# Block 2's gate products spread over its attention, with weights laid out by block and conditioning units moved

## The chip, the cores and the metric

The program runs on one core of a Trainium2 chip. Its time is the device time of one launch in microseconds (us). The engines that matter are TensorE (PE, matrix products; its weight loads are listed as PEld), VectorE (DVE), ScalarE (ACT), GpSimd (POOL) and SyncE (SP), which issues the weight loads from memory. TensorE's clock has two levels, 1.2 and 2.4 GHz; the granted clock in the rows is the share of full speed.

## The reference

Two transformer blocks run on 256 tokens of width 2048, all in fp32. Block 1: attention with a relative bias beside a pooling branch, output projection, then an up projection whose result passes a causal depthwise convolution of three taps, gelu times value, and a down projection. Block 2 is conditioned: a vector gives shifts, scales and gates through the large matrix `w_ada`.

```python
p = h @ w_in_l                              # keys, values, queries and 2 x 2048 gate columns
oa = gqa(qa, ka_all, va_all)                # 16 heads of 128, keys of context and tokens (512)
ob = diff_attn(qb, kb_all, vb_all, ...)     # 8 heads, each two softmaxes over 512 keys
merged = sigmoid(g_a) * (oa @ w_br_a) + sigmoid(g_b) * (ob @ w_br_b)
x = x + m_lat[2] * (merged @ w_out)
x = x + m_lat[5] * ((silu(h @ w_ff_gate) * (h @ w_ff_up)) @ w_ff_down)
```

## The kernel before

The kernel keeps the activations on chip, features on the partitions, and streams every weight once. A stage (`Stage`, L96) is one weight matrix or a part of it; its groups are blocks of 256 output columns, and a group is cut into units of 512 rows by 256 columns (512 KB). A unit goes through a ring of four buffers: SP loads `raw` (L374), ACT rounds it to `whi` (`hi`, L540), DVE forms the rest `wlo` (`lo`, L850), and PE does 24 products for the unit (`multiply`, L1330 to L1334), which together give an fp32 result. `raw` of a slot may be loaded again when its `wlo` is done, `whi` may be overwritten when PE has used the slot's previous unit. So the order of work on every engine is the order of units that the code writes out, and one late link holds the units behind it.

Some stages also carry conditioning items (`ada=1`): each body of two or four groups gets four extra units of `w_ada` in the ring (`ADA_AFTER`, L50). Three of them are scaled by ACT (L536, four instructions each) and added up by POOL (L408 to L419); the fourth is done by DVE alone (L842, L845). Then PE sums over partitions (L1343) and DVE stores the item (`store_mods`, L979). There are 64 items.

In the up projections DVE takes a finished group out of PSUM (L924), and applies the taps (L931 newest, L936 the two older ones, for two tiles of 128 channels each), all of it ahead of the next `lo` in DVE's order; gelu (L548) and the product with the value half follow (L968 to L974).

Between the query stage `q_rest` and the gate stages nothing is multiplied with streamed weights: key and query norms (PE L1513 and L1497, ACT L719, DVE L1224), rotations (ACT swaps L742, DVE L1214 to L1218, POOL L511 to L513), then 32 units of attention a (score L1540, maximum L1252, exp L763, scale L1248, transposes L1525, copy L771, values L1532) and 16 units of attention b (score L1567, maximum L1275, two exps L787, L1262 to L1270, copy L795, values). Then the sums for the output norm of attention b (PE L1588, one ACT square root L805) are formed, and the stages `gate_a` and `gate_b` run: 16 groups of 4 units, with 8 conditioning items. ACT writes their sigmoids (L551) to on-chip tiles. In `gate_a` DVE also normalizes the heads of b (`output_norm`, with two reciprocals a body). `branch_a` and `branch_b` follow, then `out`. PSUM has four banks `acc` (two groups of two), two `turned`, `sums` and `ada_sums`.

Of the kernel before, what the change touches and what calls it, by code (L numbers as in the profile page):

```python
# [32 lines left out]
P = 128  # L33
# [61 lines left out]
V_STEPS = {"scale": 0, "mix_out": 3, "conv": (6, 9), "down1": 0, "down2": 3, "kv": 0, "q": 0, "gate": 0,  # L95
           "branch_a": 0, "branch_b": 1, "out": 4, "glu": (0, 3), "down_x": 3}  # L96
A_STEPS = {"conv": (1, 0), "gate": (1, 1), "glu": (2, 1)}
# [26 lines left out]
def build(nc, xT, ctxT, vec, cst, rel, w_in, pool_w, w_o, w_up, w_down, w_ada, w_in2, w_bra, w_brb, w_out2,  # L124
          w_fg, w_fu, w_fd, out):
    km = lambda w: w.rearrange("(k p) n -> p k n", p=P)
    W = {k: km(v) for k, v in dict(w_in=w_in, w_o=w_o, w_up=w_up, w_down=w_down, w_in2=w_in2, bra=w_bra, brb=w_brb,
                                   out=w_out2, fg=w_fg, fu=w_fu, fd=w_fd).items()}
    ada_src = km(w_ada)

    def cols(w, k, c0, stride):

        return lambda b, GB, gb, u: W[w][:, k + UK * u:k + UK * u + UK, ds((b * GB + gb) * stride + c0, GW)]

    def pairs(wg, wu, g0, u0):

        return lambda b, GB, gb, u: W[(wg, wu)[gb % 2]][:, UK * u:UK * u + UK,
                                                          ds(b * GW + (g0, u0)[gb % 2], GW)]
# [6 lines left out]
    st_up1b = Stage("up1b", pairs("w_up", "w_up", 4 * GW, DFF + 4 * GW), 2 * n1 - 8, 4, "conv", tile0=8, feat0=8)  # L145
# [6 lines left out]
    st_ga = Stage("gate_a", cols("w_in2", 0, KVW + QW, GW), 8, 4, "gate", ada=1, tile0=16)  # L152
    st_gb = Stage("gate_b", cols("w_in2", 0, KVW + QW + D, GW), 8, 4, "gate", ada=1, tile0=48)
    st_ba = Stage("branch_a", cols("bra", 0, 0, GW), 8, 4, "branch_a", ada=1, op=88)
    st_bb = Stage("branch_b", cols("brb", 0, 0, GW), 8, 2, "branch_b", per_body=4, ada=1, who=1)
    st_out = Stage("out", cols("out", 0, 0, GW), 8, 4, "out", op=104)
# [5 lines left out]
    stages = number([st_in, st_o, st_up1a, st_up1b, st_dn1, st_up2, st_dn2, st_kv, st_q1, st_q2, st_ga, st_gb, st_ba, st_bb,  # L162
                     st_out, st_u1a, st_u1b, st_d1, st_u2, st_d2])

    with ExitStack() as ctx:
# [27 lines left out]
        CA = sb("cond_sums", [P, 2, GW], F32, here(2 * GW * 4))  # L193
        IO = sb("ident_ones", [P, 256], F32, here(1024))
# [17 lines left out]

        PS = ctx.enter_context(nc.psum_tensor("acc", [P, 2, 2, 512], F32))
# [55 lines left out]
        split_hi = sem("split_hi")  # L269
        out_stored = sem("out_stored")  # L270
# [24 lines left out]
        def cond_silu(st, u, x):  # L295

            k = (KT if st.ib >= ADA_CTX else 0) + UK * u + x
            return CS[:, k:k + 1]

# [54 lines left out]
        O_SRC = (8, 12, 32, 36)  # L354

# [4 lines left out]
        def _(sp):  # L360
            def load(st, b, prior):

                for j, (gb, u) in enumerate(st.entries):
                    if gb is None:
                        src = ada_src[:, UK * u:UK * u + UK,
                                      ds((b + st.ib) * GW - (ADA_CTX * GW if st.ib >= ADA_CTX else 0), GW)]
                    else:
                        src = st.src(b, st.GB, gb, u)
# [24 lines left out]
        def _(pool):  # L393
# [75 lines left out]
            add_condition(st_up1a)  # L469

# [23 lines left out]
            pool.wait_ge(ada_ops, st_ga.ib * ADA_OPS + 1)  # L494
# [19 lines left out]
            for st in (st_ga, st_gb, st_ba, st_bb, st_u1a):  # L514
# [4 lines left out]
        def _(act):  # L519
# [23 lines left out]
            def post(st, b, gb):  # L543

                g = group(st, b, gb)
                if st.kind == "conv" and gb % 2 == 0:
                    act.wait_ge(evac_done, g + 3)
                    act.activation(Gb[:], Cb[:], ACT.Gelu_apprx_tanh).then_inc(astep, 1)  # L548
                elif st.kind == "gate":
                    act.wait_ge(used, grouped(st, b, gb))  # L550
                    act.activation(R[:, ds(b * 4 + (st.tile0 + 2 * gb), 2), :], PS[:, gb % 2, :, 0:S],  # L551
                                   ACT.Sigmoid).then_inc(astep, 1)
# [5 lines left out]
            def gate_act(st, b):  # L558

                act.wait_ge(evac_done, group(st, b, 0) + 3)  # L560
                act.activation(Gb[:], Gb[:], ACT.Silu).then_inc(astep, 1)

            def body(st, b, final=False):

                for j in range(RING, RING + st.upb):
# [9 lines left out]
                    if st is st_ga and j == RING + 8:  # L575
# [1097 lines left out]
```

## Time and profile before

| | |
|---|---|
| median of 3 runs | 3146.78 us (3143.88 to 3147.21) |
| profiled execution | 3145.76 us, span 3143.9 us |
| PE, PEld busy | 2926.2 us (93%), 2699.2 us (86%) |
| DVE, ACT, POOL busy | 62%, 50%, 25% |
| moved from memory | 598.29 MB, mean 190 GB/s, most of it in packets of about 1 KB |
| mean granted PE clock | 0.97 |

A busy PE is not a PE at its peak: ends of products are modelled, so the number of products in a stretch says more than the busy share. Times in the rows are counted from the span's start. Rows of a stretch give the busy time of each engine with the number of its instructions. Rows of groups give line, engine, operation, output and input with shapes and count, then busy time, the mean of one in ns, and the idle time just before them with who ended it. An fp32 product that is not split by hand shows as two records.

### The profile page before, as it was taken

To read this page: it belongs to the slowest core of one execution; us is meant where nothing else is said; L and a number is where in the kernel's file an instruction comes from. 1 tells how busy PE (TensorE), PEld (TensorE's weight loads), DVE (VectorE), ACT (ScalarE), POOL (GpSimd) and SP (SyncE) were. 2 spreads that over 40 slices of the span, in tenths; PEclk is the share of its full clock that TensorE was granted. 3 is DMA by queue.
4 is the path that set the end of the run, shared out by engine and by line. 5 is a ranking of instruction groups with operands and counts; after the bars stand their busy time and mean duration, and the time that the engine had idled before them with its cause. 6 is when DMAs were issued, how large, how long until landed. Compare 5 with 4: busy or idle time off the path is not lost.

```text
span 3143.9 us, 57610 instructions
## 1 busy us (share of the span) xinstructions
PE 2926.2 (93%) x20282; PEld 2699.2 (86%) x20282; DVE 1946.6 (62%) x2412; ACT 1564.1 (50%) x2203; POOL 786.3 (25%) x646
## 2 busy tenths in 40 slices
PE   7998789999998997999998778999997999999999
PEld 7988789999988997788898547999996888888888
DVE  5566888776688866433456555655766665555554
ACT  5555554345565543323455645665535644334443
POOL 2554432003233321212341402445303400000000
PEclk9999899999999998999998989999998999999999
DMA  7874666657777764344574003887755865656655
GB/s 245 266 246 126 222 201 201 180 181 243 240 225 227 235 218 148 120 149 135 180 248 140 1 1 125 255 261 247 241 182 178 255 213 181 188 186 187 187 185 163
DMA packets 595176, 598.29 MB, mean 190 GB/s; under 512 B 18257, under 2 KB 593105, under 8 KB 594833
## 3 DMA queue, kind: packets, MB, share of 16 engines
q1 hardware_dynamic: 591936, 589.37, 60.3%
q10 hardware_dynamic: 2368, 4.91, 0.4%
q0 software_dynamic: 784, 2.88, 0.3%
q8 instruction: 50, 0.82, 0.1%
q14 instruction: 38, 0.30, 0.0%
HBM read 594.99 MB, written 2.10 MB: 190 GB/s over the span
## 4 chain that ended last, share of the span: by engine, by line
PE 60%; DVE 15%; DMA 10%; ACT 7%; issue 7%; DVEq 1%; ACTq 0%; SPq 0%
PE acc L1334 19%; PE acc L1330 13%; PE acc L1332 13%; PE acc L1333 12%; DVE wlo L850 5%; DMA raw<-w_ada 5%; DMA raw<-w_in 2%; ACT whi L540 2%; ACT cond_products L536 1%; DVE cond_sums L842 1%; DVE conv_out L936 1%; PE sums L1392 1%; DMA raw<-w_up 1%; DMA raw<-w_brb 1%; DVE conv_in L924 1%
## 5 line engine op out<-in xcount | busy, mean ns | idle before, releaser
L850 DVE TENSOR_TENSOR wlo<-raw,whi 128x1024 fp32r<-128x1024 f32 x864 | 1120.3, 1307 | 892.5 <-ACT whi L540 888.9
L1334 PE MATMUL acc<-operand,wlo 128*128 128x256 f32 (+1 forms) x5504 | 1606.6, 292 | 0.0
L540 ACT ACTIVATE whi<-raw 128x1024 fp32r<-128x1024 f32 x864 | 911.3, 1058 | 1096.5 <-PE acc L1334 733.5
L1332 PE MATMUL acc<-operand,whi 128*128 128x256 f32 (+1 forms) x4096 | 1222.6, 298 | 98.3 <-DVE wlo L850 63.4
L1333 PE MATMUL acc<-operand,whi 128*128 128x256 f32 (+1 forms) x4096 | 1210.7, 296 | 0.0
L1334 PEld LDWEIGHTS acc<-operand,wlo 128*128 128x128 f32 x5504 | 1063.0, 193 | 15.4
L1332 PEld LDWEIGHTS acc<-operand,whi 128*128 128x128 f32 x4096 | 795.4, 194 | 125.4 <-DVE wlo L850 56.5
L1333 PEld LDWEIGHTS acc<-operand,whi 128*128 128x128 f32 x4096 | 795.6, 194 | 15.0
L408 POOL TENSOR_TENSOR cond_products<-cond_products 128x512 f32<-128x512 f32 x192 | 252.6, 1316 | 1425.9 <-ACT cond_products L536 1424.0
L1330 PE MATMUL acc<-operand,whi 128*128 128x512 f32 x1408 | 502.9, 402 | 16.9 <-DVE wlo L850 9.0
L536 ACT ACTIVATE cond_products<-raw,cond_silu 128x256 f32<-128x256 f32 x768 | 327.8, 498 | 255.7 <-PE acc L1334 159.3
L1334 PE MATMUL acc<-ffn_act,wlo 128*128 128x256 f32 x1408 | 396.9, 282 | 0.0
L1330 PEld LDWEIGHTS acc<-operand,whi 128*128 128x128 f32 x1408 | 266.3, 189 | 86.9 <-DVE wlo L850 12.9
L1334 PEld LDWEIGHTS acc<-ffn_act,wlo 128*128 128x128 f32 x1408 | 268.1, 190 | 0.0
L1330 PE MATMUL acc<-ffn_act,whi 128*128 128x512 f32 x704 | 248.8, 399 | 0.0
L1332 PE MATMUL acc<-ffn_act,whi 128*128 128x256 f32 x704 | 200.2, 284 | 4.6 <-DVE wlo L850 4.6
L1333 PE MATMUL acc<-ffn_act,whi 128*128 128x256 f32 x704 | 199.2, 283 | 0.0
L416 POOL TENSOR_TENSOR cond_sums<-cond_sums,cond_products 128x256 f32<-128x256 f32 x128 | 163.3, 1276 | 10.0
L1330 PEld LDWEIGHTS acc<-ffn_act,whi 128*128 128x128 f32 x704 | 132.3, 188 | 33.0
L414 POOL TENSOR_TENSOR cond_products<-cond_products 128x256 f32<-128x256 f32 x128 | 151.1, 1181 | 10.0
L1332 PEld LDWEIGHTS acc<-ffn_act,whi 128*128 128x128 f32 x704 | 135.1, 192 | 5.8 <-DVE wlo L850 5.8
L1333 PEld LDWEIGHTS acc<-ffn_act,whi 128*128 128x128 f32 x704 | 135.1, 192 | 0.0
(201 smaller groups left out, 2000.0 us busy)
## 6 DMA issues: line engine op xcount, KB each, us to landing
raw<-w_ada SPq DMA_DIRECT2D x256, 512.0 KB, 4.7
raw<-w_in SPq DMA_DIRECT2D x224, 512.0 KB, 4.8
raw<-w_up SPq DMA_DIRECT2D x176, 512.0 KB, 4.8
raw<-w_down SPq DMA_DIRECT2D x88, 512.0 KB, 4.9
raw<-w_fg SPq DMA_DIRECT2D x88, 512.0 KB, 4.3
raw<-w_fu SPq DMA_DIRECT2D x88, 512.0 KB, 4.5
raw<-w_fd SPq DMA_DIRECT2D x88, 512.0 KB, 3.5
raw<-w_o SPq DMA_DIRECT2D x32, 512.0 KB, 4.8
```

The costliest lines, as they stand in the source:

```text
L408: pool.tensor_tensor(w[:, 0:2, :], w[:, 0:2, :], w[:, 2:4, :], ALU.add).then_inc(ada_ops, 1)
L414: pool.tensor_tensor(w[:, 0, :], w[:, 0, :], w[:, 1, :], ALU.add).then_inc(ada_ops, 1)
L416: pool.tensor_tensor(CA[:, 1, :], CA[:, 1, :], w[:, 0, :], ALU.add).then_inc(ada_ops, 1)
L536: ins = act.activation(prod[j % RING][:, x, :], raw[j % RING][:, x, :], ACT.Copy, scale=cond_silu(st, u, x))
L540: act.activation(whi[j % RING][:], raw[j % RING][:], ACT.Copy).then_inc(hi_done, 2 if st.entries[j % st.upb - 1] == (None, ADA_VEC) else 1)
L842: ins = dve.scalar_tensor_tensor(out=CA[:, 0, :], in0=w, scalar=c, in1=CA[:, 0, :], op0=ALU.mult, op1=ALU.add)
L850: dve.tensor_tensor(wlo[j % RING][:], raw[j % RING][:], whi[j % RING][:].bitcast(F32), ALU.subtract).then_inc(lo_done, 2 if prev[0] is Non ...
L924: did(dve.tensor_tensor(Zp[:, :, 2:S + 2], sums, rep(RS[:], 2), ALU.mult))
L1330: pe.matmul(both, h[:, x, f], mov, start=first, stop=False)
L1332: pe.matmul(out_, h[:, x, f], mov[:, 0], start=first, stop=False)
L1333: pe.matmul(out_, h[:, x, f], mov[:, 1], start=False, stop=False)
L1334: ins = pe.matmul(out_, l[:, x, f], mov[:, 0], start=False, stop=last)
```

## The change

1. `gate_a` and `gate_b` become one stage `gates` of 16 groups without conditioning, and its 64 units are written out as 64 slots. In slot s, PE first does a piece of the norms (slots 2 to 9), of attention a (slots 11 to 45) or of attention b (slots 43 to 61), then the 24 products of unit s. ACT and DVE do the same one slot ahead, with the split of unit s + 4 first. The gate sums use two PSUM banks instead of four, scores the other two. Attention b's scores have one buffer instead of two. Attention outputs go to `sums` and `ada_sums`.
2. Every fourth slot ACT takes the sigmoid of a group into a small tile `GT` and issues a store to memory (16 of 256 KB). Ahead of `branch_a` ACT issues four loads of 1 MB that bring them back; DVE waits for two of them ahead of `branch_a`'s splits, for the rest ahead of `branch_b`'s.
3. The output norm of attention b moves behind the slots: its sums are inserted after the first unit of `branch_a`, the reciprocals and splits into `branch_a`'s bodies.
4. The 8 conditioning items of the gates move to the next four bodies of block 1's up projection (`up1b`) and to `out`.
5. In all up projections the newest tap (with the bias) moves from DVE to ACT; DVE does its `lo` before the older taps.
6. The host stores each weight matrix by blocks of 256 columns, so a unit is 4 KB contiguous for each partition instead of four pieces of 1 KB.

```diff
-V_STEPS = {..., "conv": (6, 9), ...
+V_STEPS = {..., "conv": (4, 7), ...
-A_STEPS = {"conv": (1, 0), "gate": (1, 1), "glu": (2, 1)}
+A_STEPS = {"conv": (2, 1), "glu": (2, 1)}
...
+    def block_of(w, g, k):
+        return W[w][:, ds(g, 1), k:k + UK, :].rearrange("p g k c -> p (g k) c")
...
+    st_up1b = Stage("up1b", ..., 8, 4, "conv", ada=1, tile0=8, feat0=8)
+    st_up1c = Stage("up1c", ..., 2 * n1 - 16, 4, "conv", tile0=16, feat0=16)
-    st_ga = Stage("gate_a", ..., 8, 4, "gate", ada=1, tile0=16)
-    st_gb = Stage("gate_b", ..., 8, 4, "gate", ada=1, tile0=48)
+    st_g = Stage("gates", ..., 16, 4, "gate")
+    st_out = Stage("out", ..., 8, 4, "out", ada=1, op=104)
...
+        gates = nc.dram_tensor("gates_spilled", (P, 32, S), F32).ap()
... scalar
+            def newest_tap(st, b, gb):
+                act.wait_ge(vstep, vst(st, b, gb, 0))
+                for m in range(2):
+                    ins = act.activation(Cb[:, m, :], Zp[:, m, 2:S + 2], ACT.Identity, scale=V[:, ds(t2 + m, 1)],
+                                         bias=V[:, ds(tb + m, 1)])
...
+            def gate(g):
+                act.wait_ge(used, grouped(st_g, g // 2, g % 2))
+                if g:
+                    act.wait_ge(gate_out, 16 * g)
+                act.activation(GT[:], PS[:, 0, g % 2, :]..., ACT.Sigmoid).then_inc(evac_done, 1)
+            for s in SLOTS:
+                hi(...)                      # unit s + 4
+                if s % 4 == 0 and s:
+                    spill(s // 4 - 1)
+                norms(s)
+                attend_a(s + 1 - AT_A)       # copy, exp, output; AT_A = 11
+                attend_b(s + 1 - AT_B)       # AT_B = 43
+                if s % 4 == 3:
+                    gate(s // 4)
... vector
+            for s in SLOTS:
+                lo(...)                      # unit s + 4
+                norms(s)                     # key scaling, rotations
+                attend_a(s + 1 - AT_A)       # maximum, then the scaling of the unit before
+                attend_b(s + 1 - AT_B)
+            dve.wait_ge(in_ga, 32)
             run(st_ba)
+            dve.wait_ge(in_gb, 32)
             run(st_bb)
... tensor
+            for s in SLOTS:
+                if 2 <= s < 2 + NK:
+                    broadcast(s - 2)
+                if s in SUMS_AT:
+                    head_sums(NK + SUMS_AT[s])
+                attend_a(s - AT_A)           # transposes of n-2, values of n-3, score of n
+                attend_b(s - AT_B)
+                multiply(st_g, b, j, False)
+            body(st_ba, 0, insert=0)         # output_sums() behind the first unit
... host
+    by_block = lambda w: np.ascontiguousarray(
+        w.reshape(w.shape[0] // P, P, w.shape[1] // GW, GW).transpose(1, 2, 0, 3))
```

## Rows read from the trace of the kernel before

**Rows 1.** Six stretches: us, busy (x records) by engine, PE clock, DMA share, GB/s.
```profile
600.00:650.00 50.00, 50.00 (x419) 50.00 (x418) 37.84 (x58) 19.85 (x20) 0.00 (x0) 1.00 0.59 179
838.15:1116.45 278.30, 253.08 (x2004) 249.59 (x2004) 230.81 (x301) 167.00 (x236) 100.98 (x92) 0.96 0.73 228
1687.40:1918.00 230.60, 175.71 (x977) 123.89 (x975) 130.35 (x258) 132.76 (x255) 33.57 (x22) 0.86 0.03 8
1918.00:2021.50 103.50, 99.14 (x807) 98.34 (x808) 66.97 (x67) 69.15 (x100) 41.79 (x36) 0.98 0.75 234
2021.50:2116.70 95.20, 91.86 (x763) 91.35 (x761) 53.23 (x54) 58.38 (x89) 45.62 (x36) 1.00 0.85 264
2116.70:2146.50 29.80, 28.10 (x222) 28.13 (x223) 19.27 (x20) 16.46 (x24) 11.80 (x9) 0.94 0.68 209
```

**Rows 2.** PE in order of time: first scores, then one unit of attention a.
```profile
1724.41 3.76 PE L1540 MATMUL acc<-tiles 128*128 128x512 f32 x4
...
1809.86 0.66 PE L1525 MATMUL turned<-ident_ones,operand_scratch 128*128 128x128 f32 x4
...
1811.21 1.05 PE L1532 MATMUL acc<-operand_scratch,tiles 128*128 128x128 f32 x8
1812.27 0.66 PE L1525 MATMUL turned<-ident_ones,operand_scratch 128*128 128x128 f32 x4
```

**Rows 3.** PE in order of time: one unit of attention b.
```profile
1856.83 0.66 PE L1525 MATMUL turned<-ident_ones,operand_scratch 128*128 128x128 f32 x4 [0.28 <-DVE operand_scratch L1270]
1857.42 1.13 PE L1567 MATMUL acc<-tiles 64*128 64x512 f32 x4
1858.48 1.16 PE L1532 MATMUL sums<-operand_scratch,tiles 128*128 128x128 f32 x8
```

**Rows 4.** Groups on ACT between 1687.4 and 1918 us.
```profile
L763 ACT ACTIVATE operand_scratch<-acc,small,operand_scratch 128x512 f32<-128x512 f32 x32 | 24.9, 778 | 28.2 <-DVE small L1255 28.0
L787 ACT ACTIVATE operand_scratch<-acc,small,operand_scratch 128x512 f32<-128x512 f32 x32 | 24.6, 772 | 36.9 <-DVE small L1278 36.9
L771 ACT ACTIVATE operand_scratch<-turned 128x512 f32<-128x512 f32 x32 | 18.8, 586 | 0.7 <-PE turned L1525 0.7
L742 ACT ACTIVATE operand_scratch<-tiles 64x1024 f32<-64x1024 f32 x8 | 8.4, 1056 | 0.1
L787 ACT ACTIVATION_READ_ACCUMULATOR operand_scratch<-acc,small,operand_scratch 128x1 f32 x32 | 6.2, 193 | 0.0
```

**Rows 5.** Groups on ACT in the two gate stages.
```profile
L540 ACT ACTIVATE whi<-raw 128x1024 fp32r<-128x1024 f32 x64 | 67.3, 1056 | 47.1 <-DMA raw<-w_in 39.3 <-POOL cond_sums L416 4.5 <-DMA raw<-w_bra 2.1
...
L551 ACT ACTIVATE tiles<-acc 128x512 f32 x16 | 9.3, 583 | 0.0
...
L551 ACT ACT_TABLE_LOAD x4 | 5.1, 1283 | 0.1
```

**Rows 6.** Groups on DVE between 1687.4 and 1918 us.
```profile
L1252 DVE TENSOR_REDUCE small<-acc 128x1 f32<-128x512 f32 x32 | 21.9, 683 | 1.4 <-PE acc L1540 1.4
...
L1275 DVE TENSOR_REDUCE small<-acc 128x2 f32<-128x1024 f32 x16 | 19.5, 1218 | 4.2 <-PE acc L1567 4.2
```

**Rows 7.** Groups on DVE in `up2`, 838.15 to 1116.45 us.
```profile
L850 DVE TENSOR_TENSOR wlo<-raw,whi 128x1024 fp32r<-128x1024 f32 x81 | 107.9, 1352 | 36.1 <-ACT whi L540 35.8
L936 DVE SCALAR_TENSOR_TENSOR conv_out<-conv_in,vectors,conv_out 128x256 f32<-128x256 f32 x80 | 53.4, 728 | 0.0
L931 DVE TENSOR_SCALAR conv_out<-conv_in,vectors 128x256 f32<-128x256 f32 x40 | 17.8, 488 | 4.8 <-DVE conv_in L924 4.8
```

**Rows 8.** The older taps on DVE between 600 and 650 us.
```profile
L936 DVE SCALAR_TENSOR_TENSOR conv_out<-conv_in,vectors,conv_out 128x256 f32<-128x256 f32 x20 | 8.3, 481 | 0.0
```

**Rows 9.** Waits in `up2`: who waited for whom, us, times, longest.
```profile
PE acc L1332 <- DVE wlo L850: 25.2, 13, 3.0
```

**Rows 10.** DMA queues, first 22 us: packets, MB, share of 16 engines.
```profile
q10 hardware_dynamic: 2368, 4.91, 62.0%
q1 hardware_dynamic: 2502, 2.50, 33.5%
```

More of the change, by code:

```diff
@@ L151, in build @@
     st_q2 = Stage("q_rest", cols("w_in2", 0, KVW + 1024, GW), 8, 4, "q", ada=1, tile0=32)
[L152 to L156, printed above, removed]
+    st_g = Stage("gates", cols("w_in2", 0, KVW + QW, GW), 16, 4, "gate")
+    st_ba = Stage("branch_a", cols("bra", 0, 0, GW), 8, 4, "branch_a", ada=1, op=80)
+    st_bb = Stage("branch_b", cols("brb", 0, 0, GW), 8, 2, "branch_b", per_body=4, ada=1, who=1, op=96)
+    st_out = Stage("out", cols("out", 0, 0, GW), 8, 4, "out", ada=1, op=104)
     st_u1a = Stage("glu1a", pairs("fg", "fu", 0, 0), 12, 4, "glu", ada=1, op=120)
@@ L298, in cond_silu, with joined @@
             return CS[:, k:k + 1]
+        def joined(st):
+            return st.next is not None and bool(st.next.ada) == bool(st.ada) and (
+                (st.next.ib >= ADA_CTX) == (st.ib >= ADA_CTX) or not st.ada)
         def groups_before(st):
@@ L545, in post @@
                 g = group(st, b, gb)
-                if st.kind == "conv" and gb % 2 == 0:
+                if st.kind == "conv":
                     act.wait_ge(evac_done, g + 3)
                     act.activation(Gb[:], Cb[:], ACT.Gelu_apprx_tanh).then_inc(astep, 1)
[L549 to L552, printed above, removed]
                 elif st.kind == "glu":
@@ L780, in _, with norms @@
-            for i in range(NB_ + 3):
-                if i < NB_:
-                    act.wait_ge(b_neg, i + 1)
-                    if i >= 2:
-                        act.wait_ge(b_turned, i - 1)
+            LATE = {1: 2, 2: 3, 3: 4, 4: 5, 6: 10, 8: 11}
+            def norms(s):
+                if s == 0:
+                    head_root(0, 16, 80, NK + 1)
+                if s < 2:
+                    squares(NK + s)
+                elif s < 4:
+                    swap(s - 2)
+                elif s < 8:
+                    swap(NK + s - 4)
+                    squares(NK + s - 2)
+                elif s == 8:
+                    head_root(80, 112, 144, 2 * NK + 1)
@@ L1031, in body @@
                         evac(st, b, gb)
+                    if st.kind == "conv" and gb != 0 and (gb == 1 or j - RING == st.last[0] + 1):
+                        older_taps(st, b, gb or 0)
                     if gb is not None:
@@ L1037, in run @@
             def run(st):
[L1038 removed]
+                alone = not joined(st)
                 with dve.Fori(0, st.bodies - alone) as b:
@@ L1459, in _ @@
             run(st_up1a, insert=2)
-            with pe.Fori(0, st_up1b.bodies - 1) as b:
-                body(st_up1b, b)
-            body(st_up1b, st_up1b.bodies - 1, insert=3)
+            run(st_up1b)
+            with pe.Fori(0, st_up1c.bodies - 1) as b:
+                body(st_up1c, b)
+            body(st_up1c, st_up1c.bodies - 1, insert=3)
             run(st_dn1)
@@ new lines, in output_sums @@
+            def output_sums():
+                pe.wait_ge(o_sq, 1)
+                for t, sums in enumerate((TP[:, 0, :], TP[:, 1, :], NB[:, :], AB[:, :])):
+                    ins = pe.matmul(sums.rearrange("p (a n) -> p a n", a=2), ones, R[:, 64 + 2 * t:66 + 2 * t, :],
+                                    start=True, stop=True)
+                ins.then_inc(o_sum, 1)
+            body(st_ba, 0, insert=0)
+            with pe.Fori(1, st_ba.bodies) as b:
+                body(st_ba, b, fresh=False)
```

450 lines of the change are left out of this document (249 added, 201 removed).

## The prediction

> **What bounds the kernel now.** I read the table of stretches first, because it counts products. Undisturbed, PE does 419 products in 50 us, that is 2.86 us for a unit of 24 and 22.9 us for a body of 8 [rows 1]; the four small products of a conditioning item add about 0.5 us, so a body with one can't be shorter than 23.4 us. The second gate stage stands at 95.2 / 4 = 23.8 us a body, so nearly at this floor. Three places are far from it. `up2` takes 278.3 / 10 = 27.8 us a body, 4.4 above it [rows 1]. The stretch from the last query unit to the first gate unit is 230.6 us in which almost nothing is loaded (DMA share 0.03) and PE's clock is 0.86 of full, so at its lower level for part of the time [rows 1]. And each hand-over between stages costs some us: `branch_a`'s first body takes 29.8 us where 23.8 would do [rows 1].
>
> In order of time PE shows the reason for the second: a unit of attention a is 2.41 us of PE work when nothing waits (1809.86 to 1812.27) [rows 2], a unit of b is 1.65 us of transposes and scores and 1.06 us of values, 2.71 us [rows 2, 3]. The 32 + 16 units are thus 77 + 43 = 120 us of PE work, but from the first score to the first gate product pass 1918.0 - 1724.4 = 194 us [rows 1, 2]. The groups on ACT and DVE say what it waits for: exps that wait for the negated maximum (28.0 and 36.9 us) [rows 4]. For `up2` the groups on DVE and the table of waits agree: DVE is busy 230.8 of 278.3 us, 23.1 a body, almost PE's own floor [rows 1], and PE stood still 13 times for a late `wlo`, 25.2 us in all [rows 9]; each such stop is followed by a spell at the lower clock.
>
> **The change part by part.** *Norms, attention and gates* took 230.6 + 103.5 + 95.2 = 429.3 us [rows 1]. After the change PE has 64 x 2.86 = 183 us of gate products, 32 x 2.41 = 77, 16 x 2.71 = 43 and about 21 us for norm sums and broadcasts (256 small records; the eight of a unit's values take 0.13 us each [rows 2], most of these are smaller, and I take 0.08): 324 us is the floor. The ceiling without any overlap is 230.6 + 183 = 414. Between them:
>
> Slots 0 to 10 hold the norms. They are a chain that passes from engine to engine (swap on ACT, rotation on DVE, a swap that needs the tile a rotation frees, squares, sums on PE, root on ACT). Before, this chain took 1687.4 to 1724.4, 37 us [rows 1, 2]. PE's own work in these slots is 31 + 21 = 52 us; chain and products in a row would be 68. ACT's swap of query chunk 8 waits for a rotation that now stands behind the last key scaling and a `lo`, and each following slot puts a `hi`, a `lo` and once a sigmoid into the chain, so I take 68, the upper bound.
>
> Slots 11 to 42 each hold 2.86 + 2.41 = 5.27 us of PE. ACT has a split of 1.06, a copy of 0.59, an exp of 0.78 with 0.19 for its sum, 0.2 of outputs; every fourth slot also a sigmoid of 0.58 between two table loads of 1.28 [rows 4, 5]: 3.6 us on average. DVE has 1.35 [rows 7], a maximum of 0.68 [rows 6] and under 1.2 of small work. Transposes of unit n come two slots after its score, copies one slot before values, so a sigmoid that makes ACT 1 us late is absorbed. Only the first eight slots, where six late swaps stand in ACT's order (four pieces each, of 1.06 us where they have 1024 elements [rows 4], 4.2 us in two slots, and of about 0.63 where they have 512, 2.5 us in four), exceed PE: ACT 47.5 against 42.2 us, so +5. Sum 32 x 5.27 + 5 = 174.
>
> Slots 43 to 58 hold 2.86 + 2.71 = 5.57 us. Here the score buffer is single: next scores wait for both exps. From the start of a slot: 2.7 to the score's end, 1.4 for the maximum of 1.22 and its scaling [rows 6], 1.9 for two exps, 6.2 in all; the next score is due at 5.57 + 1.65 = 7.2. That holds with 1 us to spare. After a sigmoid it doesn't: load, sigmoid, `hi`, then `lo` ahead of DVE's maximum, and the exp ends near 14.3 where 12.8 is due. With 1.5 to 1.8 us for each of four sigmoids: 16 x 5.57 + 7 = 96. The last five slots are 14.3 + 4.3 = 19 us. Section: 68 + 174 + 96 + 19 = 357, a gain of 72.
>
> A rule of the Trainium skill speaks against this part ("ScalarE: Activation LUTs", "What ACT_TABLE_LOAD costs"): it counts a drain of some 1.38 us besides the load of 1.28 for each switch of table set, and advises to batch by set. The trace shows 1283 ns for the load [rows 5]; with the page's drain this estimate would come out 22 us longer (it is a rival below).
>
> *The hand-over to `branch_a`.* ACT has the last sigmoid (0.6), the square of 2048 elements (about twice a split less its fixed part, 1.9) and a split (1.06) before DVE's 1.3: PE idles some 6 us, then starts at the lower clock, and 8 records of output sums come in (2 us by the four records of 1.06 us in [rows 3], up to 5 at the lower clock). The four loads of 1 MB are issued between the splits; 2 MB for `branch_a`'s wait land about 12 to 18 us after the last product, the splits that wait are due after 23, so I cost them nothing; without that cover they cost up to 5 us. First body 35 instead of 29.8: +5.5. The output norm's reciprocals make `gate_a` 8.3 us longer than `gate_b` together with its slow start [rows 1]; half of that moves to `branch_a`: +4.
>
> *Conditioning items.* In `out`, four bodies get 0.5 us of PE work and as much of friction (23.8 against 22.9 [rows 1]): +4. In `up1b` four bodies of 22.9 us become bodies of the `up2` kind.
>
> *Taps.* Four tap instructions of 0.49 us leave DVE per body, with the 0.5 us of idle time before them [rows 7]: DVE's 23.1 becomes 21.2, plus small gaps between dependent steps. ACT gets four of about 0.4 and has 167 of 278 us in use [rows 1]. More important is the order: the `lo` behind a group now waits for one instruction of 0.69 us, not for seven with 3 to 5 us. What remains is that the older taps then delay the next `lo`, and that they are long because POOL works beside them: 728 ns each [rows 7], 481 ns where POOL is idle [rows 8]. The Trainium skill ("SBUF — State Buffer", the term "shared port pair") says that DVE and GpSimd exclude each other on one port pair for a whole instruction, which would leave all of that delay in place. Bounds for a body are 23.4 (PE) and 27.8 (no effect); I take 25.2, nearer the floor because DVE is no longer as full as PE. Pricing `up1a` like `up2`: 14 x 2.6 = -36; `up1b`: 4 x 2.3 = +9.
>
> *Layout.* In the first 22 us, 4.91 MB in mostly larger pieces took 62.0% of 16 engines, 44 us per MB, and 2.50 MB in pieces of 1 KB 33.5%, 47 us per MB [rows 10]. A gain of 6% to perhaps 20% in the load of the queues, with a share of 0.85 where items are mixed in [rows 1], makes loads land sooner; what it can return outside the up projections is their distance to 23.4: 0.4 us a body in some 24 bodies, and about 1.4 in six of `glu1a`, 18 us. Between 0 and 18 I take -10.
>
> Sum: -72 + 5.5 + 4 + 4 + 9 - 36 - 10 = -95.5. Against the profiled execution's 3145.8 us that is 3050, and the median of the runs lies 1 us above it: 3051 us. The range of this case by itself is 3025 to 3078.
>
> **The rivals.** *Slots in series.* In every slot ACT and DVE do the split for unit s + 4 first, and that waits for PE's products of slot s. If PE's next piece needed a result of the same slot, a slot would be 5.3 + 1.06 + 1.35 + 0.85 + 0.97 + 0.8 = 10.3 us, the section 48 x 10.3 + 87 = 581, the time 3275. It makes the kernel slower once the 48 slots average above 7.7 us instead of 5.6. For it: single score buffer and one order on each engine. Against it: the offsets in the code leave a whole slot at each step but one. Chance 0.05.
>
> *Dear switches.* If each of the sigmoids' switches holds ACT 1.38 us longer, four sigmoids in b cost 11, two beside the late swaps 5, the norm chain 6: 3073. Against it: 0.1 us of idle time in all stands by the loads' row [rows 5]. Chance 0.10.
>
> *The conv stages don't move.* POOL's pieces and the length of DVE's work stay, bodies remain 27.8, and `up1b`'s four become so too: +36 + 10, 3097. Chance 0.15.
>
> *Everything is fed in time.* Earlier landings and the earlier `lo` take all 18 conv bodies to 23.5 (-31), the rest to its floor (-8), no stalls in b (-7): 3005. Chance 0.13.
>
> **How the numbers follow.** My forecast holds 0.57. The range reaches from 3004 to 3097 and leaves out the first rival and parts of the outer two. A measurement of this kernel tells 0.2% (6 us) from no change; every case but the first lies 49 us or more below, so faster 0.93, same 0.02, slower 0.05.
>
> **What the changed profile would show.** DMA share near 0.5 through the attention and a granted clock of 1.0; 24 products every 5.3 us in a and 5.6 in b; a section of 357 us from the last query unit to the last gate unit; waits of scores on the second exp only behind a sigmoid; conv bodies of 25 us with few waits for `wlo`; landings under 4.5 us. The prediction is wrong if PE waits in most slots, if the norm slots take well under 60 us, or if conv bodies stay near 27.8 or reach 23.5.

## The result and the profile after

The changed kernel takes 3087.06 us (median of 4 runs, 3086.12 to 3088.72) against 3145.33 us for the kernel before (4 runs, 3136.34 to 3147.21): ratio 0.9821, 95% interval 0.9801 to 0.9841. The forecast was 3051 us, in a range of 3004 to 3097. The kernel is faster, as said, but by 58 us (1.8%) where 95 were expected. The profiled execution took 3086.12 us, its span is 3084.3.

Time by part, from the instants at which DVE stores a conditioning item and, in the changed kernel, of ACT's last sigmoid (in brackets: body or stretch before and after):

| part | forecast | measured |
|---|---|---|
| last query item to the last gate | -72 | -48 (426.8 to 378.8) |
| from there to `branch_a`'s first item | +5.5 | +10.1 (29.8 to 39.9) |
| output norm, items in `out` | +8 | +3.4 |
| `up1a`, `up2` | -36 | -20.7 (`up2` 27.83 to 26.26 a body) |
| items in `up1b` | +9 | +17.5 (eight bodies and the step to `down1`, 222.5 to 240.0) |
| layout (`w_in`, block 1's attention, `w_o`, `glu1a`) | -10 | -9.5 |
| rest of block 2, from `glu1a`'s last item | 0 | -10.9 (609.1 to 598.1) |

The parts add up to -58.1 us, the spans differ by 59.6; the rest is spread over other stages.

Stretches of the changed kernel, columns as in [rows 1]: `up2`; from the last query item to the first score (slots 0 to 10); on to ACT's sigmoid of the group of slots 16 to 19; to that of slots 36 to 39; to the last sigmoid; `branch_a`'s first body. By the time of the first two of these sigmoids PE has also done the products of slots 20 and 40, so the third row holds ten slots of PE, 11 to 20, and the fourth twenty, 21 to 40.

```profile
843.15:1105.73 262.58, 247.82 (x2013) 242.32 (x2012) 206.51 (x261) 185.76 (x276) 117.18 (x93) 1.00 0.75 243
1679.24:1749.90 70.66, 61.28 (x521) 59.28 (x521) 38.89 (x42) 35.84 (x41) 0.00 (x0) 0.90 0.31 92
1749.90:1828.66 78.76, 56.88 (x348) 48.79 (x348) 40.13 (x49) 48.91 (x72) 35.51 (x20) 0.83 0.25 74
1828.66:1932.37 103.71, 103.19 (x765) 93.60 (x766) 51.47 (x101) 66.32 (x105) 0.18 (x1) 0.98 0.38 115
1932.37:2058.02 125.65, 117.98 (x865) 99.89 (x863) 75.33 (x128) 81.53 (x143) 0.00 (x0) 1.00 0.35 106
2058.02:2097.93 39.91, 32.77 (x235) 30.47 (x236) 26.08 (x23) 24.32 (x35) 14.94 (x11) 0.91 0.78 276
```

The idea works where nothing else stands beside it: in the fourth and fifth row PE is busy 221 of 229 us, and four slots of attention a take 20.24 us, 5.06 each. The third row is the exception: in ten slots PE works 57 of 79 us, at a mean granted clock of 0.83. POOL is at work there (35.5 us) and hardly anywhere else in the slots. Who waits in it (waiting line, its releaser, us in all, times, longest):

```profile
...
DVE wlo L918 <- ACT whi L554: 34.3, 8, 6.0
ACT operand_scratch L800 <- DVE small L1324: 25.9, 10, 4.3
...
PE turned L1624 <- DVE operand_scratch L1331: 15.7, 5, 7.8
```

ACT waits for DVE and DVE for ACT, and PE for DVE. One turn of it, on ACT in order of time (start, us):

```profile
1775.35 0.78 ACT L800 ACTIVATE operand_scratch<-acc,small,operand_scratch 128x512 f32<-128x512 f32 x1 [2.13 <-DVE small L1324]
1776.03 0.19 ACT L800 ACTIVATION_READ_ACCUMULATOR operand_scratch<-acc,small,operand_scratch 128x1 f32 x1
1776.25 2.54 ACT L768 ACTIVATE operand_scratch<-tiles 32x512 f32<-32x512 f32 x4
1778.82 1.06 ACT L554 ACTIVATE whi<-raw 128x1024 fp32r<-128x1024 f32 x1
...
1782.51 0.78 ACT L800 ACTIVATE operand_scratch<-acc,small,operand_scratch 128x512 f32<-128x512 f32 x1 [2.15 <-DVE small L1324]
```

and on DVE:

```profile
1779.91 1.40 DVE L918 TENSOR_TENSOR wlo<-raw,whi 128x1024 fp32r<-128x1024 f32 x1 [2.96 <-ACT whi L554]
1781.23 0.68 DVE L1321 TENSOR_REDUCE small<-acc 128x1 f32<-128x512 f32 x1
1781.95 0.53 DVE L1324 TENSOR_TENSOR small<-small,operand_scratch 128x1 f32<-128x1 f32 x1
```

From exp to exp pass 7.16 us: exp 0.97, a late exchange 2.54, split 1.06, then DVE's `lo` 1.40, the maximum 0.68, its scaling 0.53. Every step follows its forerunner with no gap. The exchange counts in full, because DVE does `lo` ahead of the maximum and `lo` waits for the split, which waits for the exchange. I had added the exchange to ACT's load alone.

### The profile page after: what moved, and what is told of

The parts are those of the page before. It is cut to its first block, busy times and chain, and to the rows that moved or that the text cites. A ratio compares the mean times of both kernels' runs of the same rounds, so it can differ in the third digit from the quotient of the medians.

```text
span 3084.3 us, 57401 instructions
## 1 busy us (share of the span) xinstructions
PE 2889.3 (94%) x20282; PEld 2679.1 (87%) x20282; DVE 1920.5 (62%) x2324; ACT 1626.7 (53%) x2312; POOL 806.3 (26%) x646
## 3 DMA queue, kind: packets, MB, share of 16 engines
q1 hardware_dynamic: 161856, 589.37, 60.7%
## 4 chain that ended last, share of the span: by engine, by line
PE 67%; DVE 11%; ACT 9%; issue 6%; DMA 5%; ACTq 1%; DVEq 0%; SPq 0%
PE acc L1431 19%; PE acc L1427 14%; PE acc L1429 13%; PE acc L1430 12%; DVE wlo L918 4%; ACT whi L554 4%; DMA raw<-w_ada 3%; ACT cond_products L550 2%; PE acc L1419 1%; DVE conv_out L1006 1%; PE acc L1421 1%; PE acc L1422 1%; DMA raw<-w_up 1%; PE sums L1492 1%; PE acc L1639 1%
## 5 line engine op out<-in xcount | busy, mean ns | idle before, releaser
L918 DVE TENSOR_TENSOR wlo<-raw,whi 128x1024 fp32r<-128x1024 f32 x864 | 1131.7, 1319 | 952.3 <-ACT whi L554 950.6
L1431 PE MATMUL acc<-operand,wlo 128*128 128x256 f32 (+1 forms) x4992 | 1452.8, 291 | 0.0
L1429 PE MATMUL acc<-operand,whi 128*128 128x256 f32 (+1 forms) x3584 | 1073.8, 300 | 94.4 <-DVE wlo L918 58.4
L1430 PE MATMUL acc<-operand,whi 128*128 128x256 f32 (+1 forms) x3584 | 1060.4, 296 | 0.0
L1431 PEld LDWEIGHTS acc<-operand,wlo 128*128 128x128 f32 x4992 | 957.8, 192 | 15.4
L1429 PEld LDWEIGHTS acc<-operand,whi 128*128 128x128 f32 x3584 | 691.1, 193 | 124.0 <-issue 55.3
L1430 PEld LDWEIGHTS acc<-operand,whi 128*128 128x128 f32 x3584 | 691.6, 193 | 15.3 <-issue 0.2
L1427 PE MATMUL acc<-operand,whi 128*128 128x512 f32 x1408 | 495.9, 398 | 13.5 <-DVE operand L1241 7.7
L1427 PEld LDWEIGHTS acc<-operand,whi 128*128 128x128 f32 x1408 | 266.2, 189 | 79.0 <-DVE wlo L918 8.7
L428 POOL TENSOR_TENSOR cond_sums<-cond_sums,cond_products 128x256 f32<-128x256 f32 x128 | 174.3, 1362 | 10.0
L1419 PE MATMUL acc<-operand,whi 128*128 128x256 f32 x512 | 164.2, 321 | 2.2 <-issue 2.2
L1427 PEld LDWEIGHTS acc<-ffn_act,whi 128*128 128x128 f32 x704 | 132.0, 188 | 30.7
L426 POOL TENSOR_TENSOR cond_products<-cond_products 128x256 f32<-128x256 f32 x128 | 144.6, 1130 | 10.0
L1421 PE MATMUL acc<-operand,whi 128*128 128x256 f32 x512 | 146.9, 287 | 0.0
```

The lines of the kernel that those rows point to most:

```text
L426: pool.tensor_tensor(w[:, 0, :], w[:, 0, :], w[:, 1, :], ALU.add).then_inc(ada_ops, 1)
L428: pool.tensor_tensor(CA[:, 1, :], CA[:, 1, :], w[:, 0, :], ALU.add).then_inc(ada_ops, 1)
L918: dve.tensor_tensor(wlo[j % RING][:], raw[j % RING][:], whi[j % RING][:].bitcast(F32), ALU.subtract).then_inc(lo_done, 2 if prev[0] is Non ...
L1419: pe.matmul(half, h[:, x, f], mov[:, 0], start=first and m == 0, stop=False, skip_group_check=True)
L1421: pe.matmul(half, h[:, x, f], mov[:, 1], start=False, stop=False, skip_group_check=True)
L1427: pe.matmul(both, h[:, x, f], mov, start=first, stop=False)
```

## The experiments

Times of a stretch are those of the profiled execution. "The stretch" is that from the last query item to `branch_a`'s first: 456.6 us before, 418.7 in the changed kernel. Each of the twelve kernels ran on one chip together with the kernel before, and its ratio is to those runs. Groups of four slots are counted from sigmoid to sigmoid on ACT.

**1. Layout alone.** The kernel before with weights stored by blocks of 256 columns.

```diff
-    km = lambda w: w.rearrange("(k p) n -> p k n", p=P)
...
+    def block_of(w, g, k):
+        return W[w][:, ds(g, 1), k:k + UK, :].rearrange("p g k c -> p (g k) c")
```

> The kernel before with part 6 alone: every weight matrix stored by blocks of 256 columns. My theory (a small help to the stages with conditioning items): 10 us less than before, between 4 and 18, all of it in bodies with items; bodies of the second gate stage 23.8 become 23.4 us, up2 27.8 becomes 27.0 to 27.5. Rival A, from the trace after the change: the last two thirds of block 2, where PE is never late, run 290 records in 50 us instead of 285 (10.9 us over the last 609 us), and the layout is the reason: then this kernel too has 290 records in 50 us there and is 20 to 30 us faster. Rival B, the 290 belong to that chip or execution and not to the layout: this kernel has the same rate there as its neighbours in this call.

Ratio 0.9973 (0.9950 to 0.9995), 8.5 us, with an interval from 1.6 to 15.7 us. `up2` stays at 27.9 us a body (27.0 to 27.5 expected), `glu1a` goes from 24.4 to 23.8 a body, `w_in` from 23.8 to 23.5, but `up1a` as a whole is 6.4 us longer. The profiled execution is 13.8 us shorter, and 10.8 of it lie in the end of block 2, which goes at another rate by itself (last section). So the median agrees with the 10 us of the sum, what the layout gives stage by stage isn't settled, and nothing of `up2`'s gain is its work.

**2. Taps alone.** The kernel before with the newest tap on ACT and `lo` ahead of the older taps.

> The kernel before with part 5 alone: the newest tap on ACT, the split ahead of the older taps. The prediction took 2.6 us off each of 14 bodies, 36 us. After the change the bodies of up2 stood at 26.3 (1.57 less) and those of up1a at 25.3, 22 us in all. Theory: nearly all of that is this edit, 15 to 20 us faster, up2 bodies 26.5. Rival: half of it comes from the layout (earlier landings), then this kernel is 8 to 12 us faster and up2 bodies are 27.0.

Ratio 0.9923 (0.9898 to 0.9947), 24 us. `up2` 26.4 us a body, `up1a` 25.5, the unconditioned `up1b` as before (222.7 against 222.5). These 1.4 us of a body of `up2` are nearly all of the 1.6 that it gains in the changed kernel, and 1.2 less than the forecast 2.6.

**3. Attention ahead of `lo` on DVE.** The changed kernel, with two statements of DVE's slot in the other order.

```diff
             for s in SLOTS:
+                if s + 1 >= AT_A:
+                    attend_a(s + 1 - AT_A)
+                    attend_b(s + 1 - AT_B)
                 lo(...)
                 norms(s)
-                attend_a(s + 1 - AT_A)
-                attend_b(s + 1 - AT_B)
```

> The changed kernel with one edit: in the slots with attention DVE takes the maximum and the scaling first and forms the weight split of unit s + 4 after them. After the change slots 11 to 19 took 78 us where 52 were forecast, and four exps in a row stand 7.15 us apart, which is the sum of exp 0.97, swap 2.54, hi 1.06 on ACT and wlo 1.38, maximum 0.68, scaling 0.53 on DVE. Theory (ACT and DVE hand one thread to and fro, the split stands in it): without the split and its hi in the thread these slots fall to about 5.3 to 6.0 us, 10 to 18 us less in all, and the stall of attention b after a sigmoid (24.23 us for four slots, 22.3 without) shrinks too, 4 to 7 us: 14 to 25 us faster than the changed kernel. Rival (POOL's rotations block DVE, ACT is simply full): 0 to 6 us faster.

Ratio 0.9751 (0.9697 to 0.9804); the stretch is 390.6 us, 28.1 shorter. On the same chip the medians of this kernel and the changed one (experiment 4) are 3066.96 and 3093.76 us. ACT, now with the exchange between two exps and no wait:

```profile
1764.41 0.78 ACT L800 ACTIVATE operand_scratch<-acc,small,operand_scratch 128x512 f32<-128x512 f32 x1
1765.08 0.19 ACT L800 ACTIVATION_READ_ACCUMULATOR operand_scratch<-acc,small,operand_scratch 128x1 f32 x1
1765.30 2.55 ACT L768 ACTIVATE operand_scratch<-tiles 32x512 f32<-32x512 f32 x4
1767.88 1.06 ACT L554 ACTIVATE whi<-raw 128x1024 fp32r<-128x1024 f32 x1
1768.84 0.58 ACT L794 ACTIVATE operand_scratch<-turned 128x512 f32<-128x512 f32 x1
1769.32 0.77 ACT L800 ACTIVATE operand_scratch<-acc,small,operand_scratch 128x512 f32<-128x512 f32 x1
```

4.91 us from exp to exp, not 7.16: `lo` and maximum lie beside ACT's work. The same ten slots of PE as a stretch (it starts 2 us behind the first score):

```profile
1749.50:1806.44 56.94, 49.34 (x347) 43.75 (x345) 38.90 (x47) 48.40 (x71) 33.55 (x19) 0.96 0.32 93
```

57 us, 59 from the first score on, instead of 79 for as many products, and 0.96 of the clock instead of 0.83. In attention b a slot goes from 6.06 to 5.71 us. The 28 us are 20 in these slots, 6 in slots 40 to 63 and 3 ahead of the first score. The same work in another order on one engine is worth as much as the section and the hand-over together had missed (24 and 4.6 us).

**4. The changed kernel again**, on the chip of experiments 1 to 3.

> The changed kernel as it is, so that the others of this call can be held against it on the same chip: 3087 us within 6, and the rate of the unhindered part of block 2 (290 records in 50 us if it belongs to the layout, 285 if it belongs to the chip).

Ratio 0.9848 (0.9807 to 0.9888); the stretch is 418.7 us again, and the gates in it come within 0.1 us of the first execution. Stretches of single profiles can thus be compared.

**5. Rotations ahead of `lo` too.** Experiment 3, and from slot 6 on DVE's `norms(s)` ahead of `lo`.

> Base: the changed kernel with attention's small steps ahead of the split on DVE (the run before this one, in which the stretch from the last query item to branch_a's first item took 390.6 us). Here DVE also does the key scaling and the rotations of slots 6 to 9 ahead of its split. Theory (the norm slots are one thread through ACT and DVE): in slots 6 and 7 ACT's exchange waited 6.1 and 4.9 us for a rotation that stood behind DVE's split, and the split behind ACT's; without that, slots 0 to 10 go from 73 to about 63 us and the stretch from 390.6 to 381. Rival (the norm slots are held by PE's small records, broadcasts and sums of 2 to 3.6 us each): the waits move to PE's sums and the stretch stays at 388 to 391.

Ratio 0.9702 (0.9642 to 0.9762), the stretch 380.6 us (381 by the theory). Of the two waits of ACT for a rotation, in experiment 3

```profile
1724.12 2.12 ACT L768 ACTIVATE operand_scratch<-tiles 64x1024 f32<-64x1024 f32 x2 [6.08 <-DVE tiles L1282]
...
1733.16 2.12 ACT L768 ACTIVATE operand_scratch<-tiles 64x1024 f32<-64x1024 f32 x2 [4.89 <-DVE tiles L1282]
```

the second nearly goes, the first stays:

```profile
1720.02 2.12 ACT L768 ACTIVATE operand_scratch<-tiles 64x1024 f32<-64x1024 f32 x2 [5.71 <-DVE tiles L1282]
```

**6. One piece of the late exchanges to a slot.** Experiment 5, with the 24 pieces in 24 slots.

```diff
-                if n in LATE:
-                    swap(LATE[n])
+                if 1 <= n <= 24:
+                    swap_piece(LATE[(n - 1) // 4], (n - 1) % 4)
```

> The norm_first kernel with the six late exchanges (24 pieces) one piece to a slot in slots 11 to 34, not four pieces in each of six slots. Theory (in slots 11 to 19 a slot is exp, exchange, split on ACT, then maximum on DVE, in a ring): 0.63 us or 1.06 us a slot instead of 2.55 or 4.26 fits beside PE's 5.06 us, so these nine slots go from 56 to about 48 us, the stretch 6 to 8 us shorter than norm_first's. Rival (DVE is late there because POOL's rotations lengthen its work): POOL's work is only spread out, no gain or 2 us. Time of the whole kernel 0.972 of the kernel before by the theory.

Ratio 0.9710 (0.9663 to 0.9756), the stretch 378.3 us: 2.4 shorter, where 6 to 8 were expected. Slots 8 to 23 gain 7.9 us (each group of four at 20.3 or below), slots 24 to 39 lose 6.5 (20.67, 21.61, 23.93, 21.25 instead of 20.24 each). The expectation had no such loss; experiment 11 asks for its cause.

**7. Late exchanges cut down.** The changed kernel with one plain copy of a chunk in place of the four pieces; it leaves out the exchange of the halves.

> The changed kernel itself, but each of the six late exchanges is one plain copy of all 128 partitions (0.59 or 1.06 us) instead of four pieces (2.55 or 4.26): the partner halves are not exchanged, the rest, POOL's rotations included, stays. Theory (serial ring through ACT and DVE): slots 11 to 19 get shorter by what leaves ACT, four times 2.0 and twice 3.2, 14 us, so from 78 to 64 us. Rival (POOL beside DVE, or PE): 78 stays within 2 us.

Ratio 0.9794 (0.9729 to 0.9859), the stretch 403.4 us. Slots 12 to 19 take 53.0 instead of 65.2 us, slots 8 to 11, with the first exchange, 22.7 instead of 27.8: 17 us for 14 us less of ACT's work, and 15 in the stretch. What ACT does there counts fully, as the ring says. POOL's rotations stayed, so they are not the main cause in these slots.

**8. A copy in place of the sigmoid.** Experiment 3 with a plain copy where the gates need a sigmoid, so that ACT has one table load left in the slots' attention where there were 27 loads.

> The kernel with attention first on DVE (390.6 us in the stretch), with a plain copy in place of the 16 sigmoids, so that ACT switches no table inside the slots (about 27 loads of 1283 ns less, 35 us of ACT's time). Theory (the switches lie beside PE's work but for a few in attention b and beside the exchanges): the stretch gets 2 to 6 us shorter. Rival of the prediction (dear switches, each with a drain of 1.38 us besides): 20 us or more shorter.

Ratio 0.9734 (0.9675 to 0.9793). The stretch is 388.4 us against 390.6: 2.2 us for 26 loads. The groups of attention b are the same to 0.1 us (22.6 to 22.8 in both). The loads in the changed kernel:

```profile
L840 ACT ACT_TABLE_LOAD x14 | 18.0, 1283 | 0.2
L800 ACT ACT_TABLE_LOAD x9 | 11.5, 1283 | 0.2
L827 ACT ACT_TABLE_LOAD x4 | 5.1, 1283 | 0.1
```

35 us of ACT's time, 0.5 us of idle time ahead of them; with attention first on DVE all but 2 us lie beside PE's work. "Dear switches" is excluded. The drain of 1.38 us that the Trainium skill states besides the load ("ScalarE: Activation LUTs", "What ACT_TABLE_LOAD costs") doesn't show in ACT's rows: 27 of them would be 37 us, an estimate by that page's figure, and the idle time ahead of the loads is 0.5 us; the load itself, 1283 ns, agrees.

**9. `branch_a`'s splits in slots 60 to 63.** Experiment 5; a quarter of the operand is formed as soon as the last group's unit has read it.

```diff
+                if s >= 60:
+                    c = s - 60
+                    act.activation(XC[:, 4 * c:4 * c + 4, 0, 0, :], R[:, O_SRC[c]:O_SRC[c] + 4, :],
+                                   ACT.Copy).then_inc(split_hi, 1)
...
```

> The norm_first kernel with the splits of branch_a's operand moved into slots 60 to 63: as soon as the gate products no longer read a quarter of the operand, ACT and DVE form that quarter for branch_a. Theory (the hand-over is ACT's last sigmoid, square and split and DVE's difference in a row, in which PE stood 6.65 us and then began at the lower clock): PE's wait falls below 1 us, the first unit runs at full clock, and the stretch from the last query item to branch_a's first goes from 380.7 to about 372. Rival (branch_a's first body is held by the square roots of the output norm, which wait for PE's sums and hold ACT's splits of weights behind them): the gain at the start is given back there, 378 to 381.

Ratio 0.9687 (0.9654 to 0.9720), the stretch 375.7 us against 380.7, between the two expectations. PE's first product of `branch_a` in experiment 5

```profile
2022.13 0.55 PE L1433 MATMUL acc<-operand,whi 128*128 128x256 f32 x1 [6.65 <-DVE operand L1375]
```

and here:

```profile
2027.61 0.39 PE L1435 MATMUL acc<-operand,whi 128*128 128x256 f32 x1 [2.64 <-ACT gate_out L840]
```

The wait falls by 4.0 us and another takes its place: the product waits for the last sigmoid, which stands behind a split on ACT (experiment 12 takes it from there).

**10. Less work on POOL.** The changed kernel with POOL's additions for block 1's items cut to 16 or 32 columns; it leaves out the rest of those sums.

```diff
-                        pool.tensor_tensor(w[:, 0:2, :], w[:, 0:2, :], w[:, 2:4, :], ALU.add)...
+                        pool.tensor_tensor(w[:, 0:2, 0:wd], w[:, 0:2, 0:wd], w[:, 2:4, 0:wd], ALU.add)...
```

> The changed kernel itself, with POOL's additions for the conditioning items cut from 256 or 512 columns to 16 or 32 in the stages up to up2 (their sums are then mostly zero; everything that the items load, that ACT and DVE do for them and that PE does stays). Theory (the conv bodies with items stay long because POOL's work beside DVE lengthens the latter's steps and holds the ring's buffers): up2's bodies go from 26.3 us to 24.5, and the older taps from 579 to 480 ns. Rival (what holds these bodies is the landing of the loads, which ACT waits for): bodies stay at 25.8 or more though DVE's steps get shorter.

`up2`, as a stretch and by DVE's groups, in the changed kernel (the stretch stands above) and here:

```profile
L918 DVE TENSOR_TENSOR wlo<-raw,whi 128x1024 fp32r<-128x1024 f32 x81 | 111.6, 1388 | 49.2 <-ACT whi L554 49.2
...
L1006 DVE SCALAR_TENSOR_TENSOR conv_out<-conv_in,vectors,conv_out 128x256 f32<-128x256 f32 x80 | 41.6, 579 | 2.9 <-ACT conv_out L579 2.9
```

```profile
828.77:1074.74 245.97, 242.91 (x2012) 241.21 (x2011) 177.53 (x261) 184.14 (x276) 39.74 (x93) 1.00 0.80 260
```

```profile
L921 DVE TENSOR_TENSOR wlo<-raw,whi 128x1024 fp32r<-128x1024 f32 x81 | 98.7, 1228 | 62.7 <-ACT whi L557 62.4
L1009 DVE SCALAR_TENSOR_TENSOR conv_out<-conv_in,vectors,conv_out 128x256 f32<-128x256 f32 x80 | 33.4, 479 | 1.3 <-ACT conv_out L582 1.1
```

Ratio 0.9732 (0.9693 to 0.9770). 24.6 us a body where the changed kernel has 26.3, with the taps at 479 ns, not 579. The 77 us that left POOL made this stage 16.6 us shorter. ACT waits for landings longer than before (35 us against 24) without harm, so the loads aren't the bound.

**11. The exchanges paced.** Experiment 9; the small pieces two to a slot, the large ones one to a slot, none beside a sigmoid.

> The early_split kernel with the late exchanges paced: the sixteen pieces of 32x512 two to a slot, the eight of 32x1024 one to a slot, none in a slot with a sigmoid (slots 11 to 33). One piece in every slot gave 11 us up to slot 23 and lost 7 after it, where pieces of 1.06 us met sigmoids. Theory (ACT's load of a single slot must stay under PE's 5.06 us): all groups of slots from 11 to 42 take 20.2 to 20.6 us, the stretch 4 to 7 us shorter than early_split's. Rival (the losses were POOL's longer rotations beside DVE, not the meeting with sigmoids): the losses of 1 to 4 us a group stay and the stretch equals early_split's within 2 us. Whole kernel about 0.967 of the kernel before by the theory.

Ratio 0.9703 (0.9672 to 0.9735), the stretch 373.2 us, 2.5 shorter than in experiment 9 where 4 to 7 were expected. Slots 24 to 35 again lose (22.45, 21.25, 21.51), though no piece meets a sigmoid, so that cause falls. DVE between 1835 and 1890 us in experiment 5, where POOL is idle by then,

```profile
L918 DVE TENSOR_TENSOR wlo<-raw,whi 128x1024 fp32r<-128x1024 f32 x11 | 13.4, 1219 | 0.0
L1331 DVE TENSOR_SCALAR operand_scratch<-operand_scratch,small 128x512 f32<-128x512 f32 x11 | 5.4, 487 | 0.4
```

and here, with POOL's rotations of 2.4 us each beside it:

```profile
L933 DVE TENSOR_TENSOR wlo<-raw,whi 128x1024 fp32r<-128x1024 f32 x11 | 15.5, 1413 | 0.0
...
L1346 DVE TENSOR_SCALAR operand_scratch<-operand_scratch,small 128x512 f32<-128x512 f32 x11 | 9.6, 871 | 0.4
```

DVE's scaling takes 871 instead of 487 ns, and PE, which never waits in that window of experiment 5, waits 4.1 us for it. This agrees with the rival: spreading ACT's pieces also moves POOL's rotations, and these still cost. A run with the two large rotations on DVE, or without them, was not tried.

**12. All of it together**, with the last sigmoid ahead of the last split.

> All that shortened the section in one kernel: attention and rotations ahead of the split on DVE, the splits of branch_a's operand in slots 60 to 63, the late exchanges paced, and in slot 63 the sigmoid ahead of the split, since PE's first product of branch_a then waited 2.64 us for that sigmoid. Theory (that wait is the sigmoid behind a split of 1.06 us): the wait becomes 1.6 us and the stretch 372 us. Rival (the sigmoid waits for the last gate product, not for the split): the wait stays at 2.6 and the stretch at 373.2. The whole kernel is expected at 0.967 to 0.972 of the kernel before, some 40 us under the changed kernel.

PE's wait is 1.69 us, the stretch 370.1 us, 2 us under the theory's. 3050.40 us (median of 6 runs), ratio 0.9704 (0.9677 to 0.9731), against 0.9821 for the changed kernel. Experiments 5, 6, 9 and 11 lie within its interval, so as whole kernels they aren't told apart; their stretches are.

## Why the prediction was right, and where it was wrong

*The number.* 3087 lies outside the 3025 to 3078 that I gave this case by itself. It is inside the whole range only through the room left for a rival that didn't happen, "the conv stages don't move". And 10.9 us of the profiled gain come from a part of the program that the change doesn't touch. That the time fell into the range is thus in part luck.

*Direction and mechanism.* PE stood for some 70 us in the attention (194 us for 120 of work [rows 1, 2]) and now works there: right. "Slots in series" is excluded by 5.06 us a slot in most of attention a, "the conv stages don't move" by experiment 2, "everything is fed in time" by 26.3 us a body.

*Slots 11 to 42: the step that failed.* By PE's products they took 192 us (1749.90 to 1942.13) where the sum had 174. "ACT 47.5 against 42.2 us, so +5" took the late exchanges as a load of ACT that is spread over eight slots. PE's slots 11 to 21 took 86 us where the sum had 11 x 5.27 + 5 = 63. (My expectations of experiments 3 and 7 set 78 us against 52; that stretch holds ten slots and not nine, so 58 is due there.) They are a ring through two engines, since DVE does `lo` ahead of the maximum. I had written out this ring for attention b ("`lo` ahead of DVE's maximum") and not for attention a. Experiment 3 opens it and gives back 20 us in these slots, experiment 7 shortens it and gives back some 15. That the ring's DVE steps were also lengthened by POOL (the scaling of one number 0.53 us) adds to it. From slot 22 the slot is 5.06 us and not 5.27, over 21 slots 4 us to the good: beside the 24 products a unit of attention adds 2.20 us, not the 2.41 of [rows 2].

*Slots 0 to 10.* 73 us against 68; the order on DVE is worth 8 us in slots 4 to 11 (experiment 5), so my "upper bound" wasn't one. The chain to the first exchange of chunk 8 remains.

*Attention b.* 96.6 us by PE's products for slots 43 to 58, 96 forecast. Here the mechanism was right too. From slot 46 on most slots take 5.71 us, but every fourth takes 7.10 (the first of them 7.59): after each sigmoid PE's transposes wait for DVE. In the changed kernel's table of waits:

```profile
PE turned L1624 <- DVE operand_scratch L1356: 6.2, 4, 1.9
```

These are four stops of some 1.5 us each, as the sum had it (1.5 to 1.8). The chain had two conditions, the sigmoid with its loads and `lo` ahead of DVE's maximum. With attention first on DVE all these slots take 5.71 us, with the table loads (experiment 3) and without (experiment 8), so the order alone removes the stop. The sigmoid without its loads was not tried in the changed order.

*The hand-over.* +10.1 against +5.5. PE waits 7.1 us for DVE's part of the operand (6 forecast; before, 1.7 of this stretch's 29.8 us were idle), and the output sums come on top with 3.6 us of PE, which I had put at 2 to 5. The last us goes with the granted clock, 0.91 instead of 0.94. The terms were right in kind, and +5.5 took them at their low end.

*Taps.* -20.7 against -36. The chosen value of 25.2 us, "nearer the floor because DVE is no longer as full as PE", was wrong: 26.3. The taps were 728 ns [rows 7] and are 579. I had also written that each of the 13 stops of PE in `up2` is followed by a spell at the lower clock; the trace before has 6 such spells there, of 3.4 us each. I had cited the rule that would have told and then not priced it. DVE's share fell as forecast (20.65 us a body, 21.2 expected), but what delays `lo` is DVE's steps beside POOL: with POOL's additions narrowed a body is 24.6 (experiment 10). The Trainium skill's rule ("SBUF — State Buffer", the term "shared port pair"), by which the two keep each other out for a whole instruction, agrees with this and with the four taps below.

*Items in `up1b`: the second step that failed.* +17.5 against +9, four conditioned bodies taking 112.0 us. Besides four bodies of `up2`'s kind a queue was passed: `add_condition(st_up1b)` was put on POOL ahead of its step of four instructions of 128x2048 (L489), which had run between two stages before:

```profile
510.33 11.24 POOL L476 TENSOR_TENSOR operand_scratch<-operand_scratch 128x2048 f32<-128x2048 f32 x4 [12.87 <-ACT operand_scratch L688]
```

and now falls into `up1b`'s last body, where DVE has taps to do. POOL, DVE and PE of the changed kernel:

```profile
589.81 10.27 POOL L489 TENSOR_TENSOR operand_scratch<-operand_scratch 128x2048 f32<-128x2048 f32 x4
```

```profile
588.29 9.00 DVE L1006 SCALAR_TENSOR_TENSOR conv_out<-conv_in,vectors,conv_out 128x256 f32<-128x256 f32 x4
597.21 6.23 DVE L918 TENSOR_TENSOR wlo<-raw,whi 128x1024 fp32r<-128x1024 f32 x4
```

```profile
599.54 0.58 PE L1429 MATMUL acc<-operand,whi 128*128 128x256 f32 x1 [7.99 <-DVE wlo L918]
```

Four taps that take 1.67 us alone took 9.00, about one of POOL's instructions (2.57 us) for each of them, and PE stood 7.99 us. Before, the same step cost PE one wait of 2.2 us. The four bodies took 28.5, 25.5, 25.7 and 32.3 us; in experiment 10, which narrows POOL's additions but not this step, 25.7, 24.2, 23.8 and 31.4. So the long last body isn't the items' additions. A run with the step ahead of `add_condition(st_up1b)` was not made.

*Layout, `out`.* -9.5 against -10, and +3.4 against +8. Experiment 1 has -8.5 for the layout alone, but between 1.6 and 15.7 us and with an uneven profile, so how well this term fits is not shown. In its bounds I had `glu1a` 1.4 us a body from the floor; at 24.4 it was 1.0.

*Rest of block 2.* Nothing of the change touches it and PE doesn't wait in it, yet it was 10.9 us shorter in this execution; the next section but one tells of it. Without it the profiled gain is 49 us, and the forecast was off by 46 and not by 35.

## What to carry to other kernels

When work is interleaved slot by slot, write out for each slot the ring of steps over all engines, in their program order, and not each engine's load; an independent step ahead of a dependent one on one engine can put a third engine's whole work into the ring. Let the short steps that release others go first, and the bulk work with slack of several slots last. When a step is moved in POOL's queue, look at what DVE does at the place where it will then run.

## What the runs showed of the hardware

DVE and POOL hold each other up instruction by instruction, even when POOL's instruction is long: the four taps above at 2.25 us each beside POOL's of 2.57. A DVE step on one number per partition went from 159 to 530 ns.

With pieces of 4 KB instead of 1 KB the weight queue moves the same 589.37 MB in 161856 packets instead of 591936, in the same share of the DMA engines' time (60.3% before):

```profile
q1 hardware_dynamic: 161856, 589.37, 60.7%
```

A load of 512 KB of `w_in`, `w_up` or `w_ada` lands after 4.0 to 4.4 us in the median instead of 4.7 to 4.8; in experiment 1, with the layout alone, after 4.4 to 4.5. One of `w_fg` or `w_fd` takes 4.3 and 3.5 as before. So the engines' busy share didn't foretell the landing.

The end of block 2 runs at one of two rates. On one chip, in the same 50 us of a part whose code is the same, experiment 3 and then experiment 4:

```profile
2700.00:2750.00 50.00, 50.00 (x285) 43.41 (x284) 25.15 (x27) 20.59 (x21) 0.00 (x0) 1.00 0.64 184
```

```profile
2700.00:2750.00 50.00, 50.00 (x290) 43.68 (x289) 26.84 (x31) 19.08 (x18) 0.00 (x0) 1.00 0.64 190
```

285 or 290 products, both at a granted clock of 1.00, PE never idle; the 128x512 product is 399 ns in the one and 394 in the other. Over 600 us this makes 10 to 12 us. The kernel before had 285, the changed kernel 290 to 291, but the kernel before with the layout alone or the taps alone had 290 to 291, and the narrowed POOL kernel 285. So it doesn't go with these changes. That it goes with the execution is likely and not shown by a second profile of one kernel: the six times of experiment 12 fall into two groups, 3041 to 3046 and 3055 to 3058 us. What sets it stays open.
